# Experts' weights of a mixture-of-experts layer loaded by neighbouring rows per partition

## What is computed

```python
h = rmsnorm(x, norm_ffn)                       # 512 tokens, 1024 features
g_logit = h @ w_group + b_group                # 4 groups
e_logit = h @ w_expert + b_expert              # 32 experts, 8 in each group
# each token: its best group, in it the best 2 experts, weights from two softmaxes
def run(xb, e):
    gate, up = split(xb @ w_gate_up[e], 2)     # w_gate_up[e]: 1024 x 512
    return (silu(gate) * up) @ w_down[e]       # w_down[e]: 256 x 1024
y = sum over the two experts of a token: weight * run(token, expert)
x = x + y
```

## Time and profile before

| | us |
|---|---|
| median of 3 runs | 2262.47 |
| lowest, highest run | 2261.14, 2265.35 |
| profiled execution, whole time | 2261.34 |
| profiled execution, span of the core's instructions | 2260.1 |

### The profile page before, as it was taken

One profiled execution on the slowest core, in us unless ns is written; L12 is line 12 of the kernel. 1 busy time (PEld: TensorE's weight loads), 2 busy tenths in 40 slices (PEclk: granted clock), 3 DMA queues, 4 the chain that ended last, 5 costly groups with the idle time before them and its releaser, 6 DMA issues.

```text
span 2260.1 us, 26867 instructions
## 1 busy us (share of the span) xinstructions
PE 1991.1 (88%) x10032; PEld 1579.4 (70%) x10032; DVE 1296.0 (57%) x2369; ACT 999.8 (44%) x1710; POOL 387.6 (17%) x432
## 2 busy tenths in 40 slices
PE   6979778897499999449989999999899899999997
PEld 6868657776255555247877788878778777888785
DVE  4448767664688888449774443323487834533233
ACT  3333257612188888445653432221456524332211
POOL 0122034301011111212410111000013200211001
PEclk9989989998699999769989999999999899999998
DMA  4234200144499999401102333323221123333221
GB/s 143 77 96 113 83 1 1 48 167 152 148 317 352 355 344 345 142 27 57 57 29 93 103 103 94 103 84 98 71 64 57 38 93 94 100 96 94 93 94 56
DMA packets 165354, 264.45 MB, mean 117 GB/s; under 512 B 13536, under 2 KB 93920, under 8 KB 165216
## 3 DMA queue, kind: packets, MB, share of 16 engines
q1 hardware_dynamic: 145568, 230.45, 31.0%
q10 hardware_dynamic: 14528, 23.80, 3.1%
q0 software_dynamic: 5120, 8.40, 1.1%
HBM read 254.22 MB, written 16.78 MB: 120 GB/s over the span
## 4 chain that ended last, share of the span: by engine, by line
PE 64%; DVE 7%; ACT 4%; issue 2%; POOL 1%; DMA 1%; PEld 1%; ACTq 0%; PEldq 0%; POOLq 0%; DVEq 0%
PE b L464 20%; PE b L466 19%; PE b L465 19%; ACT m L577 2%; PE b L2325 1%; PE b L2311 1%; DVE m L2521 1%; PE b L1782 1%; PE b L2345 1%; PE b L2346 1%; PE b L2347 1%; ACT m L643 1%; PE b L554 0%; ACT m L447 0%; DVE m L2549 0%
## 5 line engine op out<-in xcount | busy, mean ns | idle before, releaser
L464 PE MATMUL b<-m,m 128*128 128x512 f32 (+3 forms) x2452 | 947.0, 386 | 94.3 <-DVE m L455 35.3
L465 PE MATMUL b<-m,m 128*128 128x512 f32 (+3 forms) x2452 | 934.8, 381 | 0.0
L466 PE MATMUL b<-m,m 128*128 128x512 f32 (+3 forms) x2452 | 934.6, 381 | 0.0
L455 DVE TENSOR_TENSOR m<-m,m 128x1024 fp32r<-128x1024 f32 (+1 forms) x404 | 506.2, 1268 | 556.9 <-ACT m L447 552.6
L447 ACT ACTIVATE m<-m 128x1024 fp32r<-128x1024 f32 (+1 forms) x428 | 446.1, 1053 | 553.2 <-PE b L466 520.6
L464 PEld LDWEIGHTS b<-m,m 128*128 128x128 f32 (+1 forms) x2452 | 450.2, 184 | 217.0 <-issue 57.5
L466 PEld LDWEIGHTS b<-m,m 128*128 128x128 f32 (+1 forms) x2452 | 450.1, 184 | 106.7 <-issue 2.1
L465 PEld LDWEIGHTS b<-m,m 128*128 128x128 f32 (+1 forms) x2452 | 451.2, 184 | 95.1 <-issue 1.5
L2770 POOL TENSOR_TENSOR m<-m,m 128x512 fp32r<-128x512 f32 x44 | 71.1, 1635 | 422.1 <-ACT m L2716 422.1
L2422 ACT ACTIVATE m<-m,m 128x512 f32<-128x512 f32 x128 | 91.3, 715 | 62.0 <-DVE m L2521 62.0
L554 PE MATMUL b<-m,m 128*128 128x128 f32 x192 | 33.1, 331 | 75.8 <-ACT m L643 51.2
(11 more groups left out here) (338 smaller groups left out, 2163.2 us busy)
## 6 DMA issues: line engine op xcount, KB each, us to landing
m<-in_w_gate_up SPq DMA_DIRECT2D x64, 1024.0 KB, 6.9
m<-in_w_gu SPq DMA_DIRECT2D x88, 512.0 KB, 3.6
m<-in_w_down SPq DMA_DIRECT2D x32, 1024.0 KB, 7.4
m<-in_w_in SPq DMA_DIRECT2D x48, 512.0 KB, 3.8
m<-in_w_down SPq DMA_DIRECT2D x44, 512.0 KB, 3.8
m<-in_w_in SPq DMA_DIRECT2D x20, 448.0 KB, 3.6
m<-in_w_o SPq DMA_DIRECT2D x16, 512.0 KB, 3.8
s_gt<-m ACTq DMA_DIRECT2D x16, 256.0 KB, 2.3
```

The costliest lines, as they stand in the source:

```text
L455: e.tensor_tensor(flat(wlo[HX[i]], i), flat(raw[RX[i][0]], i), fr(flat(whi[HX[i]], i)), ALU.subtract).then_inc(sem("w_lo"), 1)
L464: e.matmul(out, xh, yh, start=start, stop=False, skip_group_check=True)
L465: e.matmul(out, xh, yl, start=False, stop=False, skip_group_check=True)
L466: return e.matmul(out, xl, yh, start=False, stop=stop, skip_group_check=True)
```

## The change

The contraction of the experts' products runs over the features in another grouping: partition p holds the features 8p to 8p+7 (for `w_down` 2p and 2p+1) in place of p, p+128, and so on. The order of the products k = 0..7 on TensorE stays. A DMA of `up` then reads 8 KB in one piece for each partition (4 neighbouring rows of 2 KB, out of 16 KB that a partition holds in all), a DMA of `down` likewise 8 KB (two rows of 4 KB).

```diff
-    def add(name, w, kt, ks, cols, cw):
+    def add(name, w, kt, ks, cols, cw, rows="(k p) n -> p k n"):
         at.setdefault(name, len(chunks))
-        v = w.rearrange("(k p) n -> p k n", p=P)
+        v = w.rearrange(rows, p=P)
...
-            add(f"up{x}", io["w_gate_up"][x], 8, 2, [0], 512)
+            add(f"up{x}", io["w_gate_up"][x], 8, 2, [0], 512, "(p k) n -> p k n")
-            add(f"down{x - 1}", io["w_down"][x - 1], 2, 1, [0], 1024)
+            add(f"down{x - 1}", io["w_down"][x - 1], 2, 1, [0], 1024, "(p k) n -> p k n")
```

The norm writes its output so that each block of 128 columns of `XN2` holds the features k, k+8, k+16, ...; it reads its inputs in memory order and writes with a step of 128 elements (512 bytes). The router's weights are loaded in the matching order:

```diff
-            e.dma_start(wr[:, :, 0:4], io["w_group"].rearrange("(k p) n -> p k n", p=P)).then_inc(sem("wr"), 16)
-            e.dma_start(wr[:, :, 4:36], io["w_expert"].rearrange("(k p) n -> p k n", p=P)).then_inc(sem("wr"), 16)
+            e.dma_start(wr[:, :, 0:4], io["w_group"].rearrange("(p k) n -> p k n", p=P)).then_inc(sem("wr"), 16)
+            e.dma_start(wr[:, :, 4:36], io["w_expert"].rearrange("(p k) n -> p k n", p=P)).then_inc(sem("wr"), 16)
...
-                    e.scalar_tensor_tensor(out=XN2[t % 2], in0=X1[:, t, :], scalar=st2[:, t:t + 1], in1=g2,
+                    e.scalar_tensor_tensor(out=XN2[t % 2].rearrange("q (k p) -> q p k", k=8), in0=X1[:, t, :].rearrange("q (p k) -> q p k", k=8),
+                                           scalar=st2[:, t:t + 1], in1=g2.rearrange("q (p k) -> q p k", k=8),
                                            op0=ALU.mult, op1=ALU.mult).then_inc(sem("n2_xn"), 1)
```

Silu reads its PSUM bank in order and writes `SG` with a step of 128 elements between the two of a pair; the product reads the bank with a step of 2 elements (8 bytes) and writes in order:

```diff
-                    e.activation(SG[i][0:CAP, :], bank[i][0:CAP, 0:256], ACT.Silu).then_inc(sem("mo_si"), 1)
+                    e.activation(SG[i][0:CAP, :].rearrange("t (f p) -> t p f", f=2), bank[i][0:CAP, 0:256].rearrange("t (p f) -> t p f", f=2), ACT.Silu).then_inc(sem("mo_si"), 1)
...
-                    e.tensor_tensor(SG[i][0:CAP, :], SG[i][0:CAP, :], bank[i][0:CAP, 256:512], ALU.mult).then_inc(sem("mo_ac"), 1)
+                    e.tensor_tensor(SG[i][0:CAP, :].rearrange("t (f p) -> t f p", f=2), SG[i][0:CAP, :].rearrange("t (f p) -> t f p", f=2),
+                                    bank[i][0:CAP, 256:512].rearrange("t (p f) -> t f p", f=2), ALU.mult).then_inc(sem("mo_ac"), 1)
```

The row numbers of the overflow table need no correction any more, and GpSimd makes them by two iotas:

```diff
-            e.wait_ge(*at("rt_io", 1))
+            e.wait_ge(*at("rt_io", 2))
             c.inc(e.tensor_copy(IOF, ti[:, 48:58]))
-            c.wait()
-            c.inc(e.tensor_scalar(IOF[:, 8:10], IOF[:, 8:10], -1024.0, None, ALU.add))
...
-            e.iota(ti[:, 48:58], pattern=[[P, 10]], base=0, channel_multiplier=1).then_inc(sem("rt_io"), 1)
+            e.iota(ti[:, 48:56], pattern=[[1, 8]], base=0, channel_multiplier=8).then_inc(sem("rt_io"), 1)
+            e.iota(ti[:, 56:58], pattern=[[P, 2]], base=0, channel_multiplier=1).then_inc(sem("rt_io"), 1)
```

## The result

| kernel | median us | range | runs |
|---|---|---|---|
| before | 2262.36 | 2256.71 to 2268.44 | 20 |
| changed | 2266.19 | 2263.67 to 2268.66 | 20 |

The ratio is 1.0016, 95% interval 1.0009 to 1.0023: +3.6 us, between +2.0 and +5.2. The forecast was 2264.6 us, +2.1, and 2266.19 lies in its range of 2254 to 2269. The profiled execution has a span of 2266.1 us, 6.0 more than that of before. Of these, 3.5 lie behind the last Silu (1341.0 us against 1337.4), where the four other profiles with the strided norm take 1337.7 to 1337.9. They belong to that one execution, so I go by the runs for the whole and by the trace for its parts.

A forecast was written before the change was run, and what follows sets the result against it. TensorE, busy 1991 of 2260 us, was taken as the bound, with the experts' loads waiting for free buffers. Norm +2.1, first expert +0.2 and L1718 -0.2 gave +2.1 on 2262.47, so 2264.6 us, range 2254 to 2269.

The forecast's parts named there:

- Bound of the stage: Experts' stage: loads run as fast as buffers come free and could move 14% more; faster loads gain zero.
- Norm, 3 x 0.71 = +2.1 us: L1585 in the routing chain: strided writes cost 0.71 us per instruction, three of four in the chain, +2.1 us.
- Silu, +0.18 us under 0.26: L1861 in each expert: strided write costs +0.18 us, hidden under 0.26 us to spare, zero in the steady state.
- its limit of 1.0 ns an element: Strided Silu in the experts: it starts to cost at 0.26 / 256 = 1.0 ns an element.
- Product, +0.18 us: L1895 in each expert: reading PSUM with a step of 8 bytes costs +0.18 us, hidden under 0.25 us, zero.
- First expert +0.2: Silu in the first expert: the stock of work beside it is not yet there, charged once, +0.2 us.
- L1718 -0.2: VectorE's correction on the way to the first tokens is removed: -0.2 us.
- free writes: Rival at the strided writes: they cost nothing, only -0.2 us is left, 2262.3 us; chance 0.28.
- the hidden limit: Rival in the experts' loads: longer pieces close the 0.23 us gap of each passage, 7.4 us, 2255.1 us; chance 0.12.
- Costly strides: Rival at norm and Silu: strided accesses cost more than Silu can hide, +14.4 us, 2276.9 at L969's median; chance 0.10.
- the ring: Experts' passage: closed loop of tokens, ScalarE's split and conversion, VectorE's low part, TensorE; 0.23 us lost each passage.
- Slow loads: Rival in the experts' loads: new address order slows them, deciding below 328 GB/s; +28 us, 2290 at 300 GB/s; chance 0.08.

The follow-up runs named there:

- loads alone: Kernel before with only the experts' loads of `up` and `down` in the new order: 2261.47 us against 2262.41, ratio 0.9998.
- the run of the steps: Kernel before plus copies and sums with various steps behind the last layer: a 16-byte SBUF step cost 0.2 us on VectorE, 0.24 on ScalarE, for 256 elements.
- The runs with the copy: One more ScalarE copy behind Silu in each expert: in the kernel before 2262.41 us against 2261.78, in the changed kernel 2268.68 us, ratio 1.0029.
- Silu alone: Kernel before with only the strided Silu and the strided product: 2262.07 us, ratio 1.0001.
- the norm alone: Kernel before with only the norm's strided write and the router's weights in the matching order: 2266.2 us, ratio 1.0015.
- TensorE reading the step: Changed kernel with norm, Silu and product in order and TensorE's transposes reading SBUF with the step: 2279.53 us, ratio 1.0078.
- the reordered one: Kernel before with the next conversion and the tokens' split ahead of Silu and the product: 2261.35 us, ratio 1.0001.
- Silu reading: Changed kernel with Silu reading PSUM with the step and writing SBUF in order: 2265.03 us, ratio 1.0015.
- the extra products: Changed kernel with 32 TensorE products into an unused bank ahead of the first transposes: 2264.6 us, ratio 1.0015.
- the two runs with four buffers: Four normed-state buffers, not two: in the kernel before with experts reordered 2259.02 us; in its own order, five small DMAs moved to SyncE, 2257.48 us.

## Why the prediction was right

- *Bound of the stage.* Right: loads alone are worth nothing, the expert takes 9.75 us, and the queue waits for VectorE.
- *Norm, 3 x 0.71 = +2.1 us.* Right in place and size: 0.72 us each, three of four in the chain, and +2.0 on the path. The price came from a row that reads SBUF with a step; that writes cost the same was not known then, and the run of the steps shows it.
- *Silu, +0.18 us under 0.26.* Right in effect, wrong in its terms. It lasts 0.26 us longer, exactly what I had called its limit of 1.0 ns an element. Read so, it would have left nothing. The runs with the copy show the terms in the engine's own time: it takes 0.15 more of a room of 0.35. Price and room were both set too small, and that the two errors cancelled was luck.
- *Product, +0.18 us.* Wrong in size, 0: PSUM read with a step is free. I had priced it by a row that reads SBUF. Nothing hung on it.
- *First expert +0.2, L1718 -0.2.* The first is right in size and wrong in cause. The first expert is 0.3 us longer, but not by Silu: with Silu alone it takes 9.7 us as before, with the norm alone 9.9. The second shows in the run of the norm alone, which keeps L1718 and is 0.2 us longer between the logits and the first split.
- *What the sum lacked.* TensorE's granted clock, which it put at nothing. The step of the prediction that fell short is that a delay of the norm passes on to the end at its own size. The logits take 7.9 to 8.0 us in six profiles with the plain norm (before, loads alone, Silu alone, TensorE reading the step, the copy in the kernel before, the reordered one), and 8.5 to 8.8 us in all five with the strided norm (changed, norm alone, Silu reading, the copy in the changed one, the extra products). That they go together is shown. It hangs on when the work comes and not on the plain norm as such, for the two runs with four buffers have the plain norm too and took 6.4 and 9.0 us. That the clock is what makes it follows from the rows of the slow products. Why the clock rises later was not settled: the run meant for it did not reach the place. The path is then +2.0 for the norm, +0.7 for the logits, +0.4 for the tables, +0.3 for the first expert and -0.2 for L1718, in all +3.2 us, where the runs measure +3.6.
- *The time as evidence.* The range, 2254 to 2269 us, also held the times of free writes and of the hidden limit, and 2.1 us lie at the lower edge of what was measured (2.0 to 5.2). The time alone would have borne out none of the three; the rows of the norm and the run of the loads alone tell them apart.
- *Rivals.* Free writes: fell, by the norm's 2.01 us. Hidden limit: fell, by the loads alone. Costly strides: the price did reach 1.0 ns on ScalarE, its point of decision, and the ring held. Slow loads: fell, 411 GB/s. The Trainium skill (DMA: Bandwidth & Descriptors, Latency and other measured facts) has half the rate lost at pitches of 4 and 8 MiB, but 207 of 214 GB/s left at 512 KiB, so it spoke for this rival even less than the prediction says. At 16 KB no loss shows here.

## What to carry to other kernels

Ask of a faster transfer who waits for it before asking how much faster it gets: a queue that waited for a buffer gave nothing back here, at a share of busy time of 0.99. If a layout needs a step somewhere, put it on a read of PSUM by ScalarE or VectorE, where a step of 8 bytes was free, and not on what the bounding engine reads; on a write to SBUF a step of 16 bytes and more cost 0.7 to 1.0 ns an element. Room beside a ring is measured from start to start, not from end to start, and a gap that is closed at one place of a ring can open at another. A delay ahead of TensorE's work can cost more, or less, than its own length, by the granted clock that the work then meets: here 1.3 us on top of 2.0.

## What I had not expected of the hardware

- The price of a step in SBUF is a threshold: 0.42 us with 8 bytes, 0.62 with 16, 0.59 with 64 (VectorE, 256 elements).
- A transpose on TensorE that reads with a step of 32 bytes takes 271 ns in place of 223, and its weight load 201 in place of 139.
- ScalarE starts its next instruction up to 0.21 us before a strided one has ended.
- The granted clock of the logits moved either way with the work ahead of them. With 5.6 us gained there, they took 1.0 us longer than before; with 1.3 us gained, by four buffers in the reordered kernel, they took 1.6 us less (6.4 us at full clock).
